# Attention with ALiBi as the bias of the exp, trimmed diagonal tiles, and block selection as a multiply on the exp's output

## The reference, cut to what matters

```
slopes = 2 ** -(1..8)
# compressed: 127 summary keys (stride 16); masked where 16c+31 > t
p_cmp = softmax(q.k_cmp*dh**-0.5 - slopes*(t - mid)) * mask;   o_cmp = p_cmp @ v_cmp
# selection, shared by the 4 heads of a group: 16 of 32 blocks of 64 keys
imp   = sum over heads of p_cmp @ overlap
score = where(block starts <= t, imp + 1000*(first, own, previous block), -1e30)
idx   = top_k(score, 16)
# selected: softmax over the keys of those blocks that are <= t
# window: softmax over keys with 0 <= t - key < 512
o = g0*o_cmp + g1*o_slc + g2*o_win
```

## Time and profile before

| | |
|---|---|
| runs | 2277.17, 2296.14, 2352.01 us; median 2296.14 |
| profiled execution | span 2277.4 us, as long as the fastest run |
| cores | 2266.4 to 2277.4 us, mean granted clock 0.938 to 0.941 |
| busy in the span | TensorE 88%, DVE 40%, ScalarE 22%, POOL 5% |
| chain that ended last | TensorE 82%, DVE 8% |
| attention | from 511.6 to 873.7 us |

### The profile page before, as it was taken

How to read it: one execution, slowest core, us unless ns; L and a number is a source line. 1 busy time by engine, 2 the same in 40 slices (tenths; PEclk the granted TensorE clock), 3 DMA queues, 4 the chain that set the end, 5 groups by cost and what they waited for, 6 DMA issues and landing times.

```text
span 2277.4 us, 31190 instructions; the slowest of 8 cores (2266.4 to 2277.4 us)
## 1 busy us (share of the span) xinstructions
PE 1998.2 (88%) x11730; PEld 1057.8 (46%) x11730; DVE 918.7 (40%) x1506; ACT 506.0 (22%) x823; POOL 118.8 (5%) x113
## 2 busy tenths in 40 slices
PE   3798879987898898865986759999999999999999
PEld 2455434443554554325873334444444444444444
DVE  3565590103324325673237761342243243144144
ACT  2232220014675673231012230000000000000000
POOL 1100100000000000000000000100100100100100
PEclk9999999968999999987997869999999999999999
DMA  9621953742000000006941123638746845844953
GB/s 226 112 91 25 114 66 38 74 56 59 1 1 1 1 2 1 1 1 200 134 75 19 19 37 37 86 47 91 90 52 82 107 51 65 111 56 56 112 74 148
DMA packets 179729, 149.09 MB, mean 65 GB/s; under 512 B 12800, under 2 KB 168832, under 8 KB 174976
## 3 DMA queue, kind: packets, MB, share of 16 engines
q0 software_dynamic: 173968, 107.13, 38.9%
q1 hardware_dynamic: 5616, 39.98, 5.0%
HBM read 245.82 MB, written 8.39 MB: 112 GB/s over the span
## 4 chain that ended last, share of the span: by engine, by line
PE 82%; DVE 8%; another core or an unknown queue 4%; issue 2%; ACT 2%; DMA 1%; POOL 1%; DVEq 0%; ACTq 0%; SPq 0%; POOLq 0%
PE bank L1124 13%; PE bank L1141 13%; PE bank L1126 13%; PE bank L485 12%; PE bank L1001 5%; PE bank L926 5%; PE bank L744 4%; PE bank L732 4%; PE bank L733 4%; PE bank L492 2%; PE bank L735 2%; DVE arena L472 2%; DVE arena L436 2%; PE bank L432 1%
## 5 line engine op out<-in xcount | busy, mean ns | idle before, releaser
L485 PE MATMUL bank<-arena 128*128 128x512 bf16 (+2 forms) x1728 | 332.7, 351 | 10.2 <-DVE arena L635 6.7
L1124 PE MATMUL bank<-arena 128*128 128x512 bf16 x1408 | 320.1, 381 | 0.0
L1126 PE MATMUL bank<-arena 128*128 128x512 bf16 x1408 | 318.3, 379 | 0.0
L1141 PE MATMUL bank<-arena 128*128 128x512 bf16 x1408 | 305.7, 379 | 0.0
L1129 DVE TENSOR_TENSOR arena<-bank,arena 128x512 bf16<-128x512 f32 x88 | 60.8, 691 | 548.8 <-PE bank L1124 443.2
L1144 DVE TENSOR_TENSOR arena<-bank,arena 128x512 f32<-128x512 f32 x352 | 243.4, 692 | 59.7 <-DVE arena L1144 41.7
L737 ACT ACTIVATE arena<-bank 128x512 bf16<-128x512 f32 x368 | 218.3, 597 | 96.8 <-PE bank L744 53.1
L485 PEld LDWEIGHTS bank<-arena 128*128 128x128 bf16 x1728 | 152.9, 99 | 179.8 <-issue 18.5
L1128 ACT ACTIVATE arena<-bank 128x512 bf16<-128x512 f32 x88 | 52.5, 597 | 824.0 <-PE bank L1124 810.8
L1124 PEld LDWEIGHTS bank<-arena 128*128 128x128 bf16 x1408 | 138.2, 98 | 167.3 <-issue 2.5
L1126 PEld LDWEIGHTS bank<-arena 128*128 128x128 bf16 x1408 | 137.8, 98 | 166.1
(11 more groups left out here) (123 smaller groups left out, 1414.9 us busy)
## 6 DMA issues: line engine op xcount, KB each, us to landing
arena<-xc SPq DMA_DIRECT2D x24, 1024.0 KB, 9.5
arena<-w_gate POOLq DMA_DIRECT2D x22, 1024.0 KB, 19.4
arena<-w_up POOLq DMA_DIRECT2D x22, 1024.0 KB, 21.9
arena<-w_down POOLq DMA_DIRECT2D x22, 1024.0 KB, 13.7
arena<-w_in POOLq DMA_DIRECT2D x18, 1024.0 KB, 12.4
arena<-w_out POOLq DMA_DIRECT2D x8, 1024.0 KB, 30.8
y<-arena SPq DMA_DIRECT2D x8, 1024.0 KB, 3.9
arena<-w_mk POOLq DMA_DIRECT2D x2, 1024.0 KB, 13.6
```

The source lines that it names most:

```text
L485: op(PE, lambda: nc.tensor.matmul(bank[psi][:, 0:n], lhsT=wt[:, kc, cc * 128:(cc + 1) * 128], rhs=actT[:, kc, t0:t0 + n], start=(kc == 0), ...
L1124: op(PE, lambda: nc.tensor.matmul(bank[pg][:, :], lhsT=wgt[:, kc, cc * 128:(cc + 1) * 128], rhs=h3T[:, kc, tc * 512:(tc + 1) * 512], start ...
L1126: op(PE, lambda: nc.tensor.matmul(bank[pu][:, :], lhsT=wut[:, kc, cc * 128:(cc + 1) * 128], rhs=h3T[:, kc, tc * 512:(tc + 1) * 512], start ...
L1141: op(PE, lambda: nc.tensor.matmul(bank[psi][:, :], lhsT=actT[a_][:, cc, tt * 128:(tt + 1) * 128], rhs=wd_[:, cc, cb4 * 512:(cb4 + 1) * 512 ...
```

## The change

ALiBi leaves the matmuls. Within one key tile, `slope * (key - t)` is split into a column per key, `slope * (key - tref)`, that the exp takes as its bias, and a factor per query that the softmax divides out. `tref` is the middle of a chunk of queries; for the steep heads 0 and 1 the chunks have 128 and 256 queries, so one tile takes up to four exps, and 512 for the others. The selection leaves the matmuls too: it is transposed, written to DRAM, read back by two DMAs that repeat each block's row over 64 partitions (`Em`, keys x queries, 0 or 1), and DVE multiplies the exp's output by it; POOL multiplies the four diagonal pieces of `Em` by a triangle. Window and selected tiles are cut to the columns that the mask leaves, with a 128-column mask matmul in window tiles. The three branches run as one stream with scores three tiles ahead, five `Pt` tiles, two `ocomb`, and the order of phases below. Transposes of a head's output come four steps after its finish, with the copy on ScalarE. The constant table shrinks from 7,329 to 1,697 columns, the 2 MB `RB` table is replaced by a 209 KB bias table, the arena grows by 6 KB and some later tiles are taken from its top end, and the memory attention has two score banks.

```diff
-        def attn_tile(Kt, Kb, Qt, Qb, LBap, RBi, mask_ap):
+        def attn_tile(Kt, Kb, h, tc, c0, c1, boff, mask, mul):
             si = rot_S.next()
-            n_extra = 1 if mask_ap is not None else 0
-            op(PE, lambda: nc.tensor.matmul(bank[si][:, :], lhsT=Kt, rhs=Qt, start=True, stop=False), r=list(Kb) + list(Qb), w=[bankb[si]])
-            op(PE, lambda: nc.tensor.matmul(bank[si][:, :], lhsT=LBap, rhs=RB[:, RBi, :], start=False, stop=(n_extra == 0)), r=[cbb, RBb[RBi]], w=[bankb[si]])
-            if mask_ap is not None:
-                op(PE, lambda: nc.tensor.matmul(bank[si][:, :], lhsT=ident, rhs=mask_ap, start=False, stop=True), r=[cbb, cidb], w=[bankb[si]])
+            op(PE, lambda: nc.tensor.matmul(bank[si][:, c0:c1], lhsT=Kt, rhs=qnT[:, h, tc * 512 + c0:tc * 512 + c1], start=True, stop=True, skip_group_check=True), r=list(Kb) + [qnTb[h][tc]], w=[bankb[si]])
+            if mask is not None:
+                m0, m1, map_ = mask
+                op(PE, lambda: nc.tensor.matmul(bank[si][:, m0:m1], lhsT=ident, rhs=map_, start=False, stop=True, skip_group_check=True), r=[cbb, cidb], w=[bankb[si]])
             pj = rot_P.next()
-            op(ACT, lambda: nc.scalar.activation(out=Pt[pj][:, :], in_=bank[si][:, :], func=AF.Exp), r=[bankb[si]], w=[Ptb[pj]])
+            cw = CHUNK[h]
+            c = c0
+            while c < c1:
+                e = min(c1, (c // cw + 1) * cw)
+                bc = boff + (tc * 512 + c) // cw
+                op(ACT, lambda: nc.scalar.activation(out=Pt[pj][:, c:e], in_=bank[si][:, c:e], func=AF.Exp, bias=biasT[:, bc:bc + 1]), r=[bankb[si], biasb], pw=[Ptb[pj]])
+                c = e
+            if mul is not None:
+                emap, embs = mul
+                op(DVE, lambda: nc.vector.tensor_tensor(out=Pt[pj][:, c0:c1], in0=Pt[pj][:, c0:c1], in1=emap, op=ALU.mult), r=embs, w=[Ptb[pj]])
             return pj
...
-            for j in range(4):
+            for j in range(c0 // 128, c1 // 128):
...
+        def topk(n):
+            tc, q = n % 2, n % 2
+            op(DVE, lambda: nc.vector.tensor_tensor(out=imp[q][:, :, :], in0=imp[q][:, :, :], in1=bonus[:, tc * 4:tc * 4 + 4, :], op=ALU.add), r=[bonusb], w=[impb[q]])
+            for j in range(4):
+                op(DVE, lambda: nc.vector.max(out=m8[:, j, 0:8], in_=imp[q][:, j, :]), r=[impb[q]], pw=[m8b])
+            for j in range(4):
+                op(DVE, lambda: nc.vector.match_replace(out=sc2[:, j, :], in_to_replace=m8[:, j, 0:8], in_values=imp[q][:, j, :], imm_value=-3.0e38), r=[impb[q], m8b], pw=[sc2b])
+            for j in range(4):
+                op(DVE, lambda: nc.vector.max(out=m8[:, j, 8:16], in_=sc2[:, j, :]), r=[sc2b], pw=[m8b])
+            for j in range(4):
...
+            def spread():
                 tb = rot_tr.next()
                 tbv = bank[tb][:, :].bitcast(BF16)
                 for j in range(4):
                     op(PE, lambda: nc.tensor.transpose(out=tbv[0:32, j * 128:(j + 1) * 128], in_=selbf[:, j, :], identity=ident), r=[selbfb, cidb], w=[bankb[tb]])
-                for hl in range(4):
-                    h = 4 * g + hl
-                    copy_op(ACT, RB[0:32, h * 2 + tc, :], tbv[0:32, 0:512], r=[bankb[tb]], w=[RBb[h * 2 + tc]])
+                op(DVE, lambda: nc.vector.tensor_copy(out=selT[0:32, :], in_=tbv[0:32, 0:512]), r=[bankb[tb]], w=[selTb])
+                dma(SP, self.sel_d[n], selT[0:32, :], r=[selTb], w=[seldb[n]])
+                nt = 12 + 4 * tc
+                for hf in range(2):
+                    src = self.sel_d[n].rearrange("(i two) q -> two i q", two=2)[hf, 0:nt, :].unsqueeze(0).broadcast_to([64, nt, 512])
+                    dma(SP, Em[q][64 * hf:64 * hf + 64, 0:nt, :], src, r=[seldb[n]], w=[Emb[q]] + Emdb[q] if hf == 0 else [], pw=[Emb[q]] + Emdb[q] if hf else [], owner=Emb[q])
+                for m in range(4):
+                    blk = Em[q][:, nt - 4 + m, m * 128:(m + 1) * 128]
+                    op(POOL, lambda: nc.gpsimd.tensor_tensor(out=blk, in0=blk, in1=tri01, op=ALU.mult), r=[cbb], w=[Emdb[q][m]])
+            at(6, spread)
...
+        def run_stream(gens, L):
+            pend = []
+            for g_ in gens:
+                for sc, pvf in g_:
+                    pend.append((pvf, sc()))
+                    if len(pend) > L:
+                        f, pj = pend.pop(0)
+                        f(pj)
+                    self.step += 1
+                    run_due()
+            while pend:
+                f, pj = pend.pop(0)
+                f(pj)
+                self.step += 1
+                run_due()
+            run_due(True)
+
+        rot_tr = Rot([7])
+        run_stream([cmp_jobs(0), win_jobs(0), cmp_jobs(1), sel_jobs(0), win_jobs(1), cmp_jobs(2), sel_jobs(1), win_jobs(2), cmp_jobs(3), sel_jobs(2), win_jobs(3), sel_jobs(3)], 3)
```

More of the change, by code:

```diff
@@ L165, in scope, with tile @@
         return Scope(self)
-    def tile(self, S, name, shape, dt):
+    def tile(self, S, name, shape, dt, hi=False):
         esz = 4 if dt == F32 else 2
@@ L743, in pv @@
+            return pj
+        def pv(pj, Ob, Vap, Vb, nv, first, c0, c1):
+            for j in range(c0 // 128, c1 // 128):
+                ob = Ob[j // 2]
                 o0 = (j % 2) * nv
-                op(PE, lambda: nc.tensor.matmul(bank[ob][:, o0:o0 + nv], lhsT=Pt[pj][:, j * 128:(j + 1) * 128], rhs=Vap, start=(first and j % 2 == 0), stop=last, skip_group_check=True), r=[Ptb[pj]] + list(Vb), w=[bankb[ob]])
-        def finish(Obanks, nv, h, tc, br, oc, mode):
-            hl = h % 4
+                op(PE, lambda: nc.tensor.matmul(bank[ob][:, o0:o0 + nv], lhsT=Pt[pj][:, j * 128:(j + 1) * 128], rhs=Vap, start=(first and j % 2 == 0), stop=True, skip_group_check=True), r=[Ptb[pj]] + list(Vb), w=[bankb[ob]])
@@ L748, in finish @@
+        def finish(Ob, nv, h, n, br, mode):
+            hl, tc, oc = h % 4, n % 2, n % 2
             rj = rot_rd.next()
@@ new lines, in finish, with at, run_due @@
+                    op(DVE, lambda: nc.vector.scalar_tensor_tensor(out=ocb[oj][:, j, :], in0=src, scalar=f, in1=acc, op0=ALU.mult, op1=ALU.add), r=[bankb[ob], rdb[rj], ocombb[oc][hl]], pw=[ocbb[oj]])
+            return oj if mode == "last" else rj
+        later = []
+        self.step = 0
+        def at(delay, fn):
+            later.append((self.step + delay, fn))
+        def run_due(everything=False):
+            due = [x for x in later if everything or x[0] <= self.step]
+            for x in due:
+                later.remove(x)
+                x[1]()
@@ new lines, in win_jobs, with sc, pvf @@
+        def win_jobs(n):
+            g, tc = n // 2, n % 2
+            for hl in range(4):
+                h = 4 * g + hl
+                Ob = rot_O.next()
+                order = [3, 0, 1, 2, 4, 5, 6, 7]
+                for k_, m in enumerate(order):
+                    i = m + 4 + 4 * tc
+                    mj = m % 4
+                    c0, c1 = (0, 128 * (mj + 1)) if m < 4 else (128 * mj, 512)
+                    mask = (128 * mj, 128 * mj + 128, wsneg if m < 4 else csneg)
+                    def sc(h=h, i=i, c0=c0, c1=c1, mask=mask):
+                        return attn_tile(KnT[:, 2 + g, i * 128:(i + 1) * 128], [KnTb[2 + g][i // 4]], h, tc, c0, c1, BOFF[h] + i * NCH[h], mask, None)
+                    def pvf(pj, h=h, i=i, c0=c0, c1=c1, Ob=Ob, k_=k_):
+                        pv(pj, Ob, Vaug[:, i, 2 + g, :], [Vaugb[i]], NV, k_ == 0, c0, c1)
+                        if k_ == 7:
+                            finish(Ob, NV, h, n, 2, "add")
+                    yield sc, pvf
```

327 lines of the change are left out of this document (120 added, 207 removed).

## The result

The changed kernel takes 2214.67 us (median of 4 runs, 2212.65 to 2278.97), the kernel before 2288.41 (median of 4): a ratio of 0.9686, 95% interval 0.9621 to 0.9751.

The account below looks back on a forecast made before the run. TensorE was taken to bound the attention stage before, ScalarE and DVE taking turns after. Terms 1 to 7 sum to 296 us against 362.1; with 4 ahead, 70 less: 2207, or 2226 by the median; middle 2216, range 2165 to 2272.

Parts of the forecast that it names:

- TensorE stops being the bound: Attention stage: TensorE work falls from 313 us busy to 140, if its clock stays at 2.4 GHz.
- Term 1: ScalarE in the attention stage: 504 biased, overlapping exps plus 16 copies to catA, 205 us; 266 with no overlap.
- Term 2: Compressed phases: ScalarE loses time while DVE does finishes and top-k, 36 us; 5.5 of it in the first phase.
- Term 3: Selected phase: a DVE finish between multiplies delays value matmuls, transposes and copy, 1.4 us per head and half, 17 us.
- Term 4: Window and selected passes of heads 2 to 7: pairs of narrow tiles don't cover the next score matmul, 10 us.
- Term 5: Ends of the stage: bias load and table load at the start, finish, transposes and copy at the end, 9 us.
- Term 6: The mask's round trip through DRAM must hide behind tiles before its selected phase; cost 0 to 5, taken as 2 us.
- Term 7: TensorE clock in the attention stage: a sixth of 368 tiles at the low level, 17 us.
- Ahead of the stage: Kernel start: the constant table shrinks from 1.77 to 0.37 MB, saving 4 us of transfers.
- (a): Rival: TensorE stays at 1.2 GHz and its 280 us bound the attention stage, total about 2260; chance 0.18.
- (c): Rival: the mask broadcast runs on one DMA engine, selected phases start 144 us late in all, total 2360; chance 0.04.
- (b): Rival: DVE becomes the bound with the multiply at 692 ns, 2231, or 2277 with exps not overlapping; chance 0.14.

Follow-up runs that it names:

- Finish in pieces: Changed kernel with a selected head's four last products given out one per tile between the next head's multiplies, its transposes three tiles later: 2203.1 us.
- wide table: Changed kernel with the 1408 KB that its constant table lost still loaded at the start, into space nothing reads: 2218.4 us (fastest run), ratio 0.9747.
- selection by matmul: Changed kernel with block selection added by a second matmul on TensorE, no mask load and no multiply: 2187.7 us (fastest run), ratio 0.9617.

## Why the prediction was right, and which of its terms were not

2216 was forecast, 2214.67 came. Part of that closeness is luck: against its own execution I forecast 70 us less and got 63, and the 9 us that I had added for the median cancelled it. The stage was to take 296 us and took 308 on the core shown, the slowest.

- **TensorE stops being the bound**: right; 209 us busy, and its score matmuls doubled cost 18.
- **Term 1 (205)**: ScalarE was busy 222. The price of a bias was right (696 ns at 512 columns for 687), but 504 exps average 530 ns, 267 us in all instead of 257 (with the copies 277, above the 240 to 260 it expected to see), and overlap by 0.106 us each (267 less 213.5 busy), not 0.12. Two exps of 512 columns back to back did overlap by 0.12 (the median of 108 pairs), but they often don't stand back to back.
- **Term 2 (36)**: mis-sized, 48. The second to fourth phase left ScalarE idle for 10.2, 12.0 and 14.8 us (19, 22 and 23 less what it was busy), the first for 11.0 beside the bias wait, where 5.5 were forecast. VectorE, busy 16 to 17 us in the second to fourth, bears out the mechanism, its finishes, and compressed tiles inside window heads give 13 us back. The multiply has a part in it: without it the waits that end these three phases were 5 us shorter in all.
- **Term 3 (17)**: the copy waited 20.0, of which 3.4 are the stage's end: 16.6. Finish in pieces shows that it is this place, the finish in front of the transposes.
- **Term 4 (10)**: size near, cause wrong. Outside the three waits that end compressed phases and count in term 2, the exps waited 9.1 us for value matmuls (22.0 less 12.9). Without the multiply, with the same narrow tiles, no wait of ScalarE between the compressed phases was longer than 0.5 us. It was VectorE's line, not narrow tiles.
- **Term 5 (9)**: 11 on this core, more than on the others: from first score to first exp 7.4 us, from the last exp to the end 3.6. The bias table took 5.6 us to land here, but 2.4 to 2.8 on the seven other cores, as forecast from pvec; there it is 4.1 us in the mean from first score to first exp, and the term some 8.
- **Term 6 (2)**: no multiply waited for the mask. Its price was wrong: the two loads of a mask ran one after the other, 13 us for the first where the sum has 4.3, and stayed hidden.
- **Term 7 (17)**: not found as a term. The clock was 0.50 to 0.69 in the compressed phases and 0.95 to 0.97 in the stretches with selected tiles. No run tells its own cost from term 2's.
- **Ahead of the stage (4)**: 4.9, and the wide table gives 4.4 of it back.

So terms 1, 2 and 5 were 31 us too small on this core, and term 7's 17 too large. What the sum did not ask is what each part is worth. Trimming gives 55 us of the stage, one stream 12 more, the exp bias 2 to 3; the multiply takes 23 back against selection by matmul.

Rivals: (a) half clock throughout and the slower (c) fall: the stretches between the compressed phases ran at 0.89 to 0.97, and the mask's loads landed in 6.5 and 8.1 us. (In (c) the third mask has 1.5 MB, so its 72 us lie under the cover of 80: 128 us of delay, not 144.) (b) falls on the price of a multiply, 427 ns.

## What to carry to other kernels

Work moved to an idle engine is paid at that engine's place in line: before adding a short operation to a chain, look for the longest block of work that can stand in front of it, and hand that block out in pieces and move back what waits for its end. When a change has several parts, price each alone; here one part gave most of the gain, and another took a third of it back unseen. Two engines that are 72% and 63% busy, as ScalarE and VectorE here, can still set the time together.

## What the runs showed of the hardware that was not expected

- One and the same 204 KB load of 128 rows took 2.4 to 2.8 us from issue to landing on seven cores and 5.6 on the eighth; the 215 KB at the kernel's start took 2.7 to 3.0 on all.
- A read that repeats each of its rows over 64 partitions moved 768 KB in 6.5 us and 1024 KB in 8.1, some 120 GB/s. While the first ran (535.3 to 542 us) the 16 DMA engines were busy 0.56 of the time in the mean, so more than one worked on it; the second load of the pair was issued when the first had landed.
- An in-place bf16 multiply in SBUF took 427 ns for 512 columns, as the bf16 copy's 422, not the f32 multiply's 692. The Trainium skill (VectorE: DVE Perf Modes, Side-by-side: where the cycles go for N=2048 bf16) lets a 16-bit operation on two tensors in SBUF do two elements a cycle behind some 158 cycles; for 512 columns that gives, as an estimate, 431 ns, and the row agrees.
